# Triangular inverse of the prompt mixing: from five Newton levels on 64x64 blocks to four on 32x32 blocks and one off-diagonal step

## The reference, cut to what matters

```python
def step(S, inp):
    r_t, w_t, k_t, v_t, kk_t, a_t = inp
    sa = jnp.einsum('bhij,bhj->bhi', S, -kk_t)
    S = S * w_t[..., None, :] + sa[..., :, None] * (kk_t * a_t)[..., None, :] + v_t[..., :, None] * k_t[..., None, :]
    return S, jnp.einsum('bhij,bhj->bhi', S, r_t)
S, ys = lax.scan(step, s0.astype(f32), xs)
```

```python
s = jnp.einsum('bqhd,bkhd->bhqk', q_nope, k_nope) + jnp.einsum('bqhr,bkr->bhqk', q_rope, k_rope)
p = jax.nn.softmax(jnp.where(mask, s * ATTN_SCALE, NEG_INF), axis=-1)
return jnp.einsum('bhqk,bkhd->bqhd', p, v)
```

## Time and profile before

| what | value |
|---|---|
| median of 3 runs | 1996.48 us (1992.92 to 1996.74) |
| profiled execution, first to last instruction (span) | 1994.1 us |
| TensorE busy | 1861.4 us, 93% |
| VectorE, ScalarE, GpSimd busy | 941.2, 670.2, 339.7 us |
| mean granted TensorE clock | 0.961 of full |

### The profile page before, as it was taken

The page is one execution under the profiler, slowest core; times in us unless marked ns, Lnnn a source line. Parts: engine busy times, 40 slices in busy tenths (PEclk is TensorE's granted clock), DMA queues, the critical chain, the costliest instruction groups (busy, mean ns, idle before and its releaser), DMA issues. The chain is left out here.

```text
span 1994.1 us, 39113 instructions
## 1 busy us (share of the span) xinstructions
PE 1861.4 (93%) x16457; PEld 1591.7 (80%) x16457; DVE 941.2 (47%) x1812; ACT 670.2 (34%) x1318; POOL 339.7 (17%) x328
## 2 busy tenths in 40 slices
PE   5999996898999899999797999999999999999997
PEld 5999994676676676666676889999899999999996
DVE  7610024457776665655343654333463333543335
ACT  2221112344444544534222023333433333433331
POOL 0000003222232222121100322100013000031000
PEclk9999996689999999998798999999999999999999
DMA  6462220100211011010517224444344444444441
GB/s 215 157 207 70 69 87 20 49 31 20 80 61 55 7 60 60 2 60 12 145 23 296 74 73 128 126 127 126 106 137 159 126 126 126 118 148 137 126 126 63
DMA packets 168064, 196.26 MB, mean 98 GB/s; under 512 B 18818, under 2 KB 142490, under 8 KB 166900
## 3 DMA queue, kind: packets, MB, share of 16 engines
q1 hardware_dynamic: 165732, 186.35, 29.8%
q0 software_dynamic: 2192, 7.93, 1.0%
HBM read 165.82 MB, written 29.25 MB: 98 GB/s over the span
## 5 line engine op out<-in xcount | busy, mean ns | idle before, releaser
L716 DVE TENSOR_TENSOR c_wo_lo<-c_raw,c_wo_hi 128x1024 fp32r<-128x1024 f32 x94 | 115.2, 1225 | 454.8 <-ACT c_wo_hi L643 454.7
L862 PE MATMUL c_pY<-c_wo_hi,c_hl 128*128 128x512 f32 x564 | 221.3, 392 | 0.0
L862 PE MATMUL c_pY<-c_wo_lo,c_hh 128*128 128x512 f32 x564 | 221.0, 392 | 0.0
L862 PE MATMUL c_pY<-c_wo_hi,c_hh 128*128 128x512 f32 x564 | 220.5, 391 | 0.0
L643 ACT ACTIVATE c_wo_hi<-c_raw 128x1024 fp32r<-128x1024 f32 x94 | 99.7, 1061 | 325.1 <-PE c_pY L862 325.1
L603 POOL TENSOR_TENSOR c_hid<-c_relu 128x384 f32<-128x384 f32 x96 | 79.5, 828 | 669.5 <-ACT c_relu L658 669.5
L894 PE MATMUL c_pU<-c_zT_hi,c_wo_hi 128*128 128x384 f32 x768 | 151.4, 338 | 1.7 <-DVE c_zT_lo L711 1.6
L894 PE MATMUL c_pU<-c_zT_lo,c_wo_hi 128*128 128x384 f32 x768 | 148.6, 334 | 0.0
L894 PE MATMUL c_pU<-c_zT_hi,c_wo_lo 128*128 128x384 f32 x768 | 148.5, 334 | 0.0
L894 PEld LDWEIGHTS c_pU<-c_zT_hi,c_wo_hi 128*128 128x128 f32 x768 | 137.7, 188 | 10.2 <-DVE c_zT_lo L711 2.7
L894 PEld LDWEIGHTS c_pU<-c_zT_hi,c_wo_lo 128*128 128x128 f32 x768 | 134.5, 188 | 0.0
(11 more groups left out here) (454 smaller groups left out, 3316.7 us busy)
## 6 DMA issues: line engine op xcount, KB each, us to landing
c_raw<-w_down SPq DMA_DIRECT2D x96, 512.0 KB, 3.6
c_raw<-w_up SPq DMA_DIRECT2D x96, 512.0 KB, 4.8
scratch_p<-a_o SPq DMA_DIRECT2D x72, 154.0 KB, 1.8
m_pr<-w_in SPq DMA_DIRECT2D x8, 1232.0 KB, 7.7
m_pr<-scratch_p SPq DMA_DIRECT2D x8, 1232.0 KB, 5.4
m_prev<-scratch_p SPq DMA_DIRECT2D x7, 896.0 KB, 4.8
scratch_h<-m_ring POOLq DMA_DIRECT2D x9, 512.0 KB, 3.9
scratch_mix<-m_ring SPq DMA_DIRECT2D x9, 512.0 KB, 2.6
```

What stands on the lines that cost most here:

```text
L716: dve.tensor_tensor(row_lo[slot_of(U)], row_raw[U % 2][:, :], row_hi[slot_of(U)].bitcast(F32), ALU.subtract).then_inc(S("row_lo"), 1)
L862: last = pe.matmul(pY[2 * t + half][:, :], x, w[:, 512 * half:512 * half + 512], start=first and a == 0, stop=final and a == 2, skip_group ...
```

## The change

Only the 64x64 inverses of the prompt mixing are made in another way. Each 64x64 triangle is split into two 32x32 triangles on the diagonal and one 32x32 block off it. The diagonal blocks, now four to a tile of 128 tokens, are inverted by four Newton levels (2, 4, 8, 16, 32 diagonals). Level 3's X step writes the result E with the orientation of every second block swapped, so that the last level can multiply the off-diagonal block LL with inverses from both sides. In the last level T4 is 16 matmuls of E with LL, which VectorE copies out negated in two instructions of 32 partitions each; X4 is 32 matmuls that write the diagonal blocks again, at a width of 64, and 16 that write the block off the diagonal; VectorE puts both into XA with one `copy_predicated`. ScalarE no longer copies the last X.

`grams` now makes the 32x32 blocks first (`gram_blocks`, 96 matmuls of 64 rows by 32 columns, which replace A and X0's product, 32 matmuls of 64 by 64), then the product for CM (`C`, 16 matmuls). The meta tile keeps its three levels. The steps of `schedule()` and the three banks are as before; T0 no longer waits for CM's masking.

```diff
@@ -988,9 +988,10 @@
+NEWTON = {META: 3, P: 4}
+HALF_CHUNK = CHUNK // 2
...
-C_LOWER, C_UPPER, C_UPPER_EQ, C_IDENT, C_UPPER_16, C_EQ_TWICE = range(N_CONST)
-C_PAIR = C_LOWER
+C_PAIR, C_UPPER, C_UPPER_EQ, C_IDENT, C_UPPER_16, C_OWN = range(N_CONST)
@@ -1181,9 +1182,13 @@
-        IA, XA, F = (sb(f"b_{n}", [P, HEADS, CHUNK]) for n in ("IA", "XA", "F"))
-        XC, QP = (sb(f"b_{n}", [P, 2, HEADS, CHUNK]) for n in ("XC", "QP"))
-        X0, CM, QM, PM = XC[:, 0], XC[:, 1], QP[:, 0], QP[:, 1]
+        XA, CM = (sb(f"b_{n}", [P, HEADS, CHUNK]) for n in ("XA", "CM"))
+        QP = sb("b_QP", [P, 2, HEADS, CHUNK])
+        QM, PM = QP[:, 0], QP[:, 1]
+        blocks = sb("b_IA", [P, 3, HEADS, HALF_CHUNK])
+        IA, LL, X0 = (blocks[:, m] for m in range(3))
+        XD, E, F = (sb(f"b_{n}", [P, HEADS, HALF_CHUNK]) for n in ("XD", "E", "F"))
@@ -1206,8 +1211,10 @@
-        low_c, up_c = (M["const"][:, C_PAIR, CHUNK * m:CHUNK * m + CHUNK] for m in range(2))
-        eq_c, twice_c = (M["const"][:, C_EQ_TWICE, CHUNK * m:CHUNK * m + CHUNK] for m in range(2))
+        own_c = M["const"][:, C_OWN, 0:3 * HALF_CHUNK].rearrange("p (x c) -> p x c", x=3)
+        one_h = M["const"][:, C_OWN, 3 * HALF_CHUNK:4 * HALF_CHUNK]
+        up_c, eq_c = (M["const"][:, C_PAIR, CHUNK * m:CHUNK * m + CHUNK] for m in range(2))
+        twice_h = M["cvec"][:, 8:8 + HALF_CHUNK]
@@ -1224,6 +1231,16 @@
+        def in_blocks(bank):
+            return bank[:, 0:W // 2].rearrange("p (h c) -> p h c", h=HEADS)
+        def n_blocks(n):
+            return 1 if n < P else P // HALF_CHUNK
+        def block_of(n, j):
+            return slice(HALF_CHUNK * j, HALF_CHUNK * j + min(n, HALF_CHUNK))
@@ -1263,7 +1280,7 @@
-                banks = [J.fill(pe, (i, jobs, 0)), spare if jobs == "A" else J.fill(pe, (i, jobs, 1))]
+                banks = [J.fill(pe, (i, jobs, g)) for g in range(2)]
@@ -1272,26 +1289,37 @@
+                for g in range(2):
+                    J.filled(ends[g])
+            def gram_blocks(i, n):
+                m = min(n, HALF_CHUNK)
+                banks = [J.fill(pe, (i, "A", 0)), spare]
+                for k in range(PAIRS):
+                    for x, (lhs, rhs) in enumerate(((KT, BT), (KT, BT), (BTn, KT))):
+                        for j in range(n_blocks(n)):
+                            B = block_of(n, j)
+                            to = block_of(n, j ^ 1) if x == 1 and n == P else B
+                            for g in range(2):
+                                r, at = slice(HD * g, HD * g + HD), HALF_CHUNK * (PAIRS * x + k)
+                                ends[g] = pe.matmul(banks[g][B, at:at + m], lhs[r, k, B], rhs[r, k, to],
+                                                    start=True, stop=True)
...
-                if jobs == "A":
-                    ends[1].then_inc(S("A1_filled"), 1)
-                else:
-                    J.filled(ends[1])
+                ends[1].then_inc(S("A1_filled"), 1)
...
-            grams = {"A": [(KT, BT)], "XC": [(BTn, KT), (khT, KT)], "QP": [(khT, RT), (BT, RT)]}
+            grams = {"C": [(khT, KT)], "QP": [(khT, RT), (BT, RT)]}
...
-            def both_chunks(i, name, v, n, lhs, rhs):
-                m = min(n, CHUNK)
-                bank = J.fill(pe, (i, name, v))
+            def each_block(bank, n, lhs, rhs, width=HALF_CHUNK):
+                m = min(n, HALF_CHUNK)
...
-                    for ck in range(1 if n < P else 2):
-                        C = rows_of(n, ck)
-                        last = pe.matmul(bank[C, CHUNK * h:CHUNK * h + m], lhs[C, h, 0:m], rhs[C, h, 0:m],
-                                         start=True, stop=True)
-                J.filled(last)
+                    for j in range(n_blocks(n)):
+                        B, at = block_of(n, j), width * h + (width - HALF_CHUNK) * (j % 2)
+                        last = pe.matmul(bank[B, at:at + m], lhs(j)[B, h, 0:m], rhs(j)[B, h, 0:m], start=True, stop=True)
+                return last
@@ -1388,15 +1416,15 @@
-                    gram(i, "XC", n)
-                    gram(i, "A", n)
+                    gram_blocks(i, n)
+                    gram(i, "C", n)
...
-                        J.wait_taken(pe, (i, "XC", g))
+                        J.wait_taken(pe, (i, "C", g))
@@ -1415,12 +1443,32 @@
-                        for g in range(2):
-                            J.wait_taken(pe, (i, "XC", g))
-                    both_chunks(i, "T", v, n, XA if v else X0, IA)
+                    bank = J.fill(pe, (i, "T", v))
+                    if v < NEWTON[n]:
+                        last = each_block(bank, n, lambda j: XD if v else X0, lambda j: IA)
+                    else:
+                        for h in range(HEADS):
+                            for j in (1, 3):
+                                last = pe.matmul(bank[block_of(n, j - 1), HALF_CHUNK * h:HALF_CHUNK * h + HALF_CHUNK],
+                                                 LL[block_of(n, j), h, :], E[block_of(n, j), h, :], start=True, stop=True)
+                    J.filled(last)
...
-                    both_chunks(i, "X", v, n, F, XA if v else X0)
+                    bank = J.fill(pe, (i, "X", v))
+                    if n < P or v < NEWTON[n] - 1:
+                        last = each_block(bank, n, lambda j: F, lambda j: XD if v else X0)
+                    elif v < NEWTON[n]:
+                        last = each_block(bank, n, lambda j: F if j % 2 else XD, lambda j: XD if j % 2 else F)
+                    else:
+                        each_block(bank, n, lambda j: F, lambda j: XD, width=CHUNK)
+                        for h in range(HEADS):
+                            for j in (0, 2):
+                                at = CHUNK * h + HALF_CHUNK
+                                last = pe.matmul(bank[block_of(n, j), at:at + HALF_CHUNK], E[block_of(n, j), h, :],
+                                                 LL[block_of(n, j), h, :], start=True, stop=True)
+                    J.filled(last)
@@ -1705,7 +1753,7 @@
-                        J.wait_filled(act, (i - 1, "XC", 1))
+                        J.wait_filled(act, (i - 1, "C", 1))
@@ -1754,8 +1802,10 @@
-                    bank, m = J.take(act, (i, "X", v)), min(n, CHUNK)
-                    J.taken(act.activation(XA[0:n, :, 0:m], heads(bank[0:n, :])[:, :, 0:m], ACT.Copy), (i, "X", v))
+                    if v < NEWTON[n]:
+                        bank, m = J.take(act, (i, "X", v)), min(n, HALF_CHUNK)
+                        to = XD if v < NEWTON[n] - 1 else E if n == P else XA
+                        J.taken(act.activation(to[0:n, :, 0:m], in_blocks(bank)[0:n, :, 0:m], ACT.Copy), (i, "X", v))
@@ -1878,12 +1928,10 @@
-                    for m in (CM, QM, PM):
-                        step(dve.memset(m, 0.0))
+                    for m in (CM, QM, PM, XA):
+                        step(dve.memset(m[:, :, :], 0.0))
...
-                        for ck in range(2):
-                            R = rows_of(P, ck)
-                            step(dve.tensor_copy(m[R, :, :], ident[R, R].unsqueeze(1).to_broadcast([CHUNK, HEADS, CHUNK])))
+                        step(dve.tensor_copy(m[:, :, :], one_h.unsqueeze(1).to_broadcast([P, HEADS, HALF_CHUNK])))
@@ -1905,7 +1953,7 @@
-                    for name, dst, mask in ((("XC", XC, up_c), ("A", IA, low_c)) if s == "grams" else (("QP", QP, eq_c),)):
+                    for name in ("A", "C") if s == "grams" else ("QP",):
@@ -1913,9 +1961,15 @@
-                                src, to = heads(bank[0:n, 0:256])[:, :, 0:m], dst[0:n, g:HEADS:2, 0:m]
-                                over = mask.bitcast(I32)[0:n, 0:m].unsqueeze(1).to_broadcast([n, PAIRS, m])
+                                m_ = min(n, HALF_CHUNK)
+                                src = bank[0:n, 0:3 * W // 4].rearrange("p (x k c) -> p x k c", x=3, k=PAIRS)[:, :, :, 0:m_]
+                                to = blocks[0:n, :, g:HEADS:2, 0:m_]
+                                over = own_c.bitcast(I32)[0:n, :, 0:m_].unsqueeze(2).to_broadcast([n, 3, PAIRS, m_])
+                            elif name == "C":
+                                src, to = heads(bank[0:n, 0:256])[:, :, 0:m], CM[0:n, g:HEADS:2, 0:m]
+                                over = up_c.bitcast(I32)[0:n, 0:m].unsqueeze(1).to_broadcast([n, PAIRS, m])
...
+                                dst, mask = QP, eq_c
@@ -1925,10 +1979,20 @@
-                    bank = J.take(dve, (i, "T", v))
-                    J.taken(dve.scalar_tensor_tensor(F[0:n, :, 0:m], heads(bank[0:n, :])[:, :, 0:m], -1.0,
-                                                     twice_c[0:n, 0:m].unsqueeze(1).to_broadcast([n, HEADS, m]),
-                                                     ALU.mult, ALU.add), (i, "T", v))
+                    bank, m = in_blocks(J.take(dve, (i, "T", v))), min(n, HALF_CHUNK)
+                    if v < NEWTON[n]:
+                        last = dve.scalar_tensor_tensor(F[0:n, :, 0:m], bank[0:n, :, 0:m], -1.0,
```

(21 more changed lines are left out.)

## The result

The changed kernel takes 2028.5 us, median of 14 runs (2014.3 to 2041.0), against 1997.4 for the kernel before, also 14 runs (1989.9 to 2016.1). The ratio is 1.015, 95% interval 1.0129 to 1.0171. The prediction was 1980 us, range 1968 to 1992: the wrong sign, and outside the range. The profiled execution of the changed kernel took 2034.1 us, 5.6 above the median.

A forecast was written before the change was run, and what follows sets the result against it. TensorE, busy 93% of the span, was taken to lead, with VectorE setting the time in one 10 us stretch. Kept savings of 20.3 us less 3 for the clock gave 17: span 1977, median 1980 us, range 1968 to 1992.

The forecast's parts named there:

- The batches, T4, X4, F: Newton steps in prompt mixing: batches and T4 0.68 us for 1.08, X4 1.36 for 1.08, VectorE's F 425 ns for 687.
- The rival that small matmuls do not get cheaper: 32-column matmuls hold the array as long as 64-column ones; 4.5 us lost, 2001 us; chance 0.03.
- Which savings arrive: Prompt mixing: savings followed by waits on ScalarE or VectorE are lost, others count; 0.40 us a batch, 0.26 each F.
- VectorE's stretch in tile 7: From F2 to the end of gate_out VectorE sets the time; 10 us before, near 9.6 us after, without a gap.
- the new copy of the last X: Moved from ScalarE to VectorE, 0.72 us, covered by VectorE idle: cost 0; rival that it comes late: 1986 us, chance 0.08.
- The kept parts: Savings that arrive, by tile: 1.84 us each in tiles 5 to 8, 2.15 in 2 and 3, 2.3 in 4.
- The products: Small products before the Newton levels: 0.65 us more a tile, free in tiles 5 to 8, costing 0.35 in 1 to 4.
- The clock: TensorE's clock falls to 0.50 behind growing waits around `lora_up`; about 1.3 us a fall, 3 us in all.
- two or three more: 3 us: Additional half-clock falls around `lora_up` in the prompt mixing, about 1.3 us each, taken off the gain.
- A mean clock under 0.95: Stated sign of being wrong: the tiles' mean TensorE clock falling below 0.95 in the profile after.
- the clock takes it back: Rival: TensorE meets the scans at half clock, 6.0 us a section; slower, 2009 us with four; chance 0.06.
- tile 1: Runs partly at half clock; four batches at 1.04 and four at 0.40, one lost, less 0.63: 5 us gain.

The follow-up runs named there:

- e6: e3 plus one unused 384-column matmul in each of two TensorE waits a tile (third head's softmax weights, decay-row transposes); 1991.7 us, ratio 0.9963.
- e3: Changed kernel's 32x32 Newton levels on the 64x64 products of the kernel before; 2002.7 us, ratio 1.0026 against the kernel before.
- e1: Kernel before plus 512 unused 32x32 and then 256 unused 64x64 matmuls ahead of the prompt mixing; 2036.3 us in its one execution.
- e2: Kernel before with the products for A and X0 made of 32x32 pieces, Newton levels untouched; 2040.5 us, ratio 1.0231.
- e8: e6 plus two more unused 384-column matmuls, ahead of the T2 batch and the decay product; 1992.5 us, ratio 0.9986 against the kernel before.
- e7: Changed kernel plus the same unused 384-column matmuls in TensorE's waits as e6; 2013.7 us, ratio 1.0081 against the kernel before.
- e5: Kernel before plus the same unused 384-column matmuls in TensorE's waits as e6; 1995.8 us, ratio 0.9992.

## Why the prediction was wrong

- **The batches, T4, X4, F: right.** 0.68, 0.62 and 1.18 us, and 0.41 to 0.43, for 0.68, 0.68, 1.36 and 0.425. The rival that small matmuls do not get cheaper is out.
- **Which savings arrive: right in sum.** The transposes in tile 5 waited 1.40 us after T1 for 1.01 before (up to 0.4 more foretold), VectorE's stretch in tile 7 lasted 9.6 us as foretold, and no wait for the new copy of the last X shows. The kept parts for tiles 2 to 8 were 2 x 2.15 + 2.3 + 4 x 1.84 + 1.3 = 15.3 us; e6's rest says 17 to 18.5, and the others 10 to 24. Single tiles differ: tile 6 of the changed kernel, at clock 1.00 in both, grew by 1.9 us with 2.9 us of idle by issue, so it kept 1.0 where 1.84 was foretold.
- **The products: the step that failed.** "That is 0.65 more. In tiles 5 to 8 it lies in a wait" priced them as array time. With the small levels they came to 17.5 us of idle by issue in seven tiles, 2.5 a tile; e3, without the small products, kept 2.9 of it. 448 instructions in one go are more than what lies ready (e1: at most 379), and the wait in tiles 5 to 8 does not hide it, since the idle also falls on the end of the step and on the batches behind it. I took the price of a small batch and of small products from the request stage without looking at what their neighbours waited for. The waits of that same stage, kernel before:

```profile
PE s_R L2211 <- issue: 4.0, 1, 4.0
PE s_R L2187 <- issue: 2.3, 1, 2.3
```

L2211 and L2187 are the very lines of the earlier trace rows. Their "issue" was on view, and I did not ask what it was. (The idle by issue in that stage was 6.4 us before and 8.8 in the changed kernel. Its code is the same in all kernels, and it ranges from 5.6 to 11.9 there, so this difference says nothing.)
- **The clock: right mechanism, wrong size.** I put "two or three more: 3 us". It cost 27 to 36 us in seven tiles, by the two prices. A mean clock under 0.95 was one of my signs of being wrong, and it was 0.93. I looked for falls at `lora_up` alone. They came there, at the waits for exponentials, behind the new idle, and three times behind no wait at all. The rival "the clock takes it back" (2009, chance 0.06) had the sign, but not the places, and knew nothing of the supply.
- **The whole.** -18.5 + 17.5 + 35.8 = 34.8 us in tiles 2 to 8 (with the lower price of the clock -10 and 27 for the outer terms). Of the other 3.4 of the 38.2, 0.3 lie ahead of tile 2 and 3.1 behind tile 8. So tile 1, from which I expected 5 us, gave none; its products have 1.6 us of idle by issue. The forecast had the first term and 3 us for the third.

Left open: how far the clock's fall in the changed kernel is the child of the supply (idle begets a fall) and how far of the smaller levels. By the median clocks of whole executions, 0.961 before, 0.948 for e3 and 0.942 for the changed kernel, about two thirds of the fall come without the supply's part. But the parts do not add: e2, with the small products alone, has 0.9515. Leaving out the 16 products of a tile that nothing uses (64 instructions) wasn't tried, since VectorE's mask would then read columns that nothing has written.

## What to carry to other kernels

Divide a change's instructions by its time before counting what it saves: here TensorE got 256 instructions in 3.45 us at best, weight loads counted, so halving the tile of a matmul is paid for as soon as a run of over a page goes below 13.5 ns an instruction. Idle put down to "issue" in the middle of a run of like matmuls is that limit, and it was in the trace of before. On a TensorE that leads, a saving that makes its waits longer can be taken back by the clock; a matmul for nothing in such a wait tells cheaply whether it is.

## What the runs showed of the hardware

- Pages of 256 TensorE instructions, 16 KB each; in a run that outpaces them one begins every 3.45 to 4.00 us, and TensorE idles 1.4 to 2.1 us in each.
- TensorE ran 379 instructions of the burst before its first stall, after a wait of 3.50 us (e1).
- The longest such idle was 6.2 us, in the request stage (changed kernel and e8). Pages come slowest where the DMA engines are busiest: 980.62 - 974.86 = 5.8 us for one in the kernel before, at a DMA share of 1.03, against 3.45 to 4.00 in e1 at 0.03. That the one causes the other is not shown.
- Matmuls whose result is not used made two kernels faster by 11 and 15 us (e6, e7) and left one as it was (e5).
- One microsecond of clock lost, (1 - clock) x time, cost 0.74 to 0.98 us of time in the kernel before, e3 and the changed kernel.
